# Three more places for weight blocks, and the first and last blocks of stages in two passes of six or seven

## The reference

```
x = x + 0.5*rms(swiglu(rms(x), w_gu, w_down))            # ffn1, hidden 2816
h = rms(x) @ w_in                                        # 14 columns of 128: xl 4, g 4, q 4, k 1, v 1
y = [rg_lru(conv(xl)) * gelu(g), window_attention(q, k, v)]   # each rms-normed
x = x + rms(y @ w_o)
x = x + 0.5*rms(swiglu(rms(x), ...))                     # ffn2
# block 2: layer_norm after each part, modulated by ada = silu(c) @ ada_w
x, ctx = retention over ctx + x (4 heads), then swiglu ffn3 on both
# block 3: only the latent
x = neighbourhood attention (16 heads, keys from x and ctx), then swiglu ffn4
```

## Time and profile before

| | |
|---|---|
| median of 3 runs | 3118.19 us (3117.08 to 3118.38) |
| the profiled execution, its own time | 3121.12 us |
| its span, first to last instruction | 3119.3 us |
| PE busy | 2943.9 us (94%) |
| DVE, ACT, POOL busy | 1505.9, 1048.2, 619.3 us |
| mean granted clock of PE | 0.97 |
| read from HBM | 262.54 MB |

### The profile page before, as it was taken

How to read it: one execution, slowest core, us unless ns; L and a number is a source line. 1 busy time by engine, 2 the same in 40 slices (tenths; PEclk the granted TensorE clock), 3 DMA queues, 4 the chain that set the end, 5 groups by cost and what they waited for, 6 DMA issues and landing times.

```text
span 3119.3 us, 39774 instructions
## 1 busy us (share of the span) xinstructions
PE 2943.9 (94%) x15968; PEld 2482.4 (80%) x15968; DVE 1505.9 (48%) x2524; ACT 1048.2 (34%) x1814; POOL 619.3 (20%) x330
## 2 busy tenths in 40 slices
PE   7999977889999999999999899999998999899997
PEld 6888965678878887868686788888896777878887
DVE  4667575555766424233232835445555535632224
ACT  4322235543232522122222541122236535442222
POOL 2333212113323110101011011111102212112221
PEclk9999998889999999999999899999998999999999
DMA  3444321014444210102011023223312111122221
GB/s 140 166 146 168 115 76 48 28 56 168 144 160 135 85 65 34 65 15 77 27 68 41 28 67 124 87 82 122 115 55 85 64 57 51 55 74 103 96 100 55
DMA packets 84697, 268.80 MB, mean 86 GB/s; under 512 B 8993, under 2 KB 16545, under 8 KB 84129
## 3 DMA queue, kind: packets, MB, share of 16 engines
q1 hardware_dynamic: 84512, 266.25, 25.0%
HBM read 262.54 MB, written 2.10 MB: 85 GB/s over the span
## 4 chain that ended last, share of the span: by engine, by line
PE 81%; DVE 10%; ACT 4%; issue 3%; POOL 1%; DMA 1%; SPq 0%; DVEq 0%; ACTq 0%; POOLq 0%
PE ps L1175 24%; PE ps L1176 24%; PE ps L1177 24%; PE ps L1362 3%; DVE t_misc L1827 2%; ACT t_whi L1444 1%; PE ps L1353 1%; DVE t_wlo L1737 1%; PE ps L1385 1%; PE ps L1412 1%; DVE t_misc L1757 1%; PE ps L1396 1%; POOL t_wlo L2166 1%; DMA t_x<-in_ctx 1%; PE ps L1265 1%
## 5 line engine op out<-in xcount | busy, mean ns | idle before, releaser
L1175 PE MATMUL ps<-t_h,t_whi 128*128 128x512 f32 (+1 forms) x2736 | 977.9, 357 | 56.2 <-DVE t_wlo L1737 29.1
L1176 PE MATMUL ps<-t_h,t_wlo 128*128 128x512 f32 (+1 forms) x2736 | 969.8, 354 | 0.0
L1177 PE MATMUL ps<-t_h,t_whi 128*128 128x512 f32 (+1 forms) x2736 | 968.7, 354 | 0.0
L2166 POOL TENSOR_TENSOR t_wlo<-t_raw,t_whi 128x1024 fp32r<-128x1024 f32 (+3 forms) x201 | 486.0, 2418 | 2083.4 <-ACT t_whi L1444 2083.4
L1175 PEld LDWEIGHTS ps<-t_h,t_whi 128*128 128x128 f32 x2736 | 527.2, 193 | 132.4 <-issue 23.0
L1737 DVE TENSOR_TENSOR t_wlo<-t_raw,t_whi 128x1024 fp32r<-128x1024 f32 (+3 forms) x201 | 253.1, 1259 | 687.3 <-ACT t_whi L1444 687.1
L1176 PEld LDWEIGHTS ps<-t_h,t_wlo 128*128 128x128 f32 x2736 | 527.2, 193 | 69.2 <-issue 1.0
L1177 PEld LDWEIGHTS ps<-t_h,t_whi 128*128 128x128 f32 x2736 | 526.6, 192 | 69.8
L1175 PE MATMUL ps<-t_hid,t_whi 128*128 128x256 f32 (+1 forms) x1648 | 536.4, 325 | 14.1 <-DVE t_hid L1869 8.5
L1444 ACT CAST t_whi<-t_raw 128x1024 fp32r<-128x1024 f32 (+3 forms) x402 | 402.1, 1002 | 402.6 <-PE ps L1177 379.0
L1176 PE MATMUL ps<-t_hid,t_wlo 128*128 128x256 f32 (+1 forms) x1648 | 531.7, 323 | 0.0
(11 more groups left out here) (225 smaller groups left out, 2473.6 us busy)
## 6 DMA issues: line engine op xcount, KB each, us to landing
t_raw<-in_gu SPq DMA_DIRECT2D x176, 512.0 KB, 3.2
t_raw<-in_ada SPq DMA_DIRECT2D x96, 512.0 KB, 3.3
t_raw<-in_dn SPq DMA_DIRECT2D x48, 448.0 KB, 3.2
t_raw<-in_dn SPq DMA_DIRECT2D x28, 512.0 KB, 3.5
t_raw<-in_ret_v SPq DMA_DIRECT2D x16, 512.0 KB, 3.2
t_raw<-in_ret_qk SPq DMA_DIRECT2D x16, 512.0 KB, 3.2
t_raw<-in_ret_g SPq DMA_DIRECT2D x16, 512.0 KB, 3.1
t_raw<-in_ret_o SPq DMA_DIRECT2D x16, 512.0 KB, 3.6
```

What stands on the lines that cost most here:

```text
L1175: e.matmul(out, whi, xlo, start=first, stop=False, skip_group_check=shared)
L1176: e.matmul(out, wlo, xhi, start=False, stop=False, skip_group_check=shared)
L1177: return e.matmul(out, whi, xhi, start=False, stop=last, skip_group_check=shared)
L2166: e.tensor_tensor(m.WLO[:, j % NH, 0:n], m.RAW[:, it.raw % NR, 0:n], m.WHI[:, j % NH, 0:n], ALU.subtract).then_inc(*S["lo_pool"].of(j))
```

## The change

Three more places for weight blocks: 4 and 5 in the context's columns of H (four pieces of 256 columns each, high halves in H's high part and low halves in its low part), and 6 in those of X, which gets a second name with the rounded type, `XW`. They are in use from the start to the start of ffn2 and from the end of the neighbourhood attention's keys to the end. `give` puts a preparation into the list with its place and the event that frees it; `over` frees a place and gives it on, or closes it, if it is one of the three and the context is about to come (`closing`).

With them: the first pass of ffn1, ffn2 and ffn4 takes six blocks instead of four (four side by side, then two one after the other), over each half, and that of the mixer seven, the four xl columns and three queries. At the end of ffn1, of ffn4 and in w_o the first of the eight last blocks is taken over all 512 tokens, and the seven others over the first half and then over the second. Ffn2's and ffn3's ends, ffn3's start and the neighbourhood attention's output columns keep batches of four. PARTS1 becomes 6, 8, 8. In the mixer the last query, the key's and the value's columns stand between the convolutions. In the neighbourhood attention the second keys come one unit earlier, and the value rows for the second half of the heads use banks 0, 1, 6, 7, 0, 1.

```diff
-PARTS1 = (7, 7, 8)
+PARTS1 = (6, 8, 8)
...
+    def give(slot, after):
+        j = next(coming)
+        where[j] = slot
+        put("prep", j=j, slot=slot, after=after)
+
     def over(j, signal, key):
-        release[j] = (signal, key)
-        put("prep", j=j + NH)
+        slot = where[j]
+        if slot in closing:
+            closing.remove(slot)
+            closed[slot] = [(signal, key)]
+        else:
+            give(slot, [(signal, key)])
...
# by_steps: blocks past the fourth, one after the other
+            for (_, _, nk, src, outs), j in zip(specs[4:], held[4:]):
+                (_, emptier, post), = outs
+                b = bank()
+                g = put("mm", w=j, slot=where[j], base=0, nk=nk, src=src, t0=t0, n=n, bank=b, po=0, before=seat(b, emptier, len(items)))
+                tick(nk * (n + 32) / 800)
+                if si == len(segs) - 1:
+                    over(j, "ps", g.id)
+                post(g)
...
# ffn(..., first=6, whole=1, begun=None)
-                together(specs[:4], subs)
-                specs = specs[4:]
+                together(specs[:first], subs)
+                specs = specs[first:]
+                if begun:
+                    begun()
...
-                last = columns(specs, ends, batch=4)
+                if whole:
+                    columns(specs[:whole], segs)
+                last = columns(specs[whole:], ends, batch=len(specs) - whole if whole else 4)
...
# the mixer
-        together([spec(c, scaled(("xl", c), MX + c * 515 + 3)) for c in range(4)], SUB1)
+        def query(c):
+            return spec(8 + c, scaled(("q", c), MQ + c * 512, 0.125))
+
+        together([spec(c, scaled(("xl", c), MX + c * 515 + 3)) for c in range(4)] + [query(c) for c in range(3)], SUB1)
         lru = recurrences()
+        others = (query(3), spec(12, scaled(("k",), MK)), spec(13, scaled(("v",), MGA + 1536)))
         for c in range(4):
             if c == 0:
                 put("conv", c=0)
             if c < 3:
                 put("conv", c=c + 1)
-            columns([spec(8 + c, scaled(("q", c), MQ + c * 512, 0.125))], SEG1)
+                columns([others[c]], SEG1)
             lru_gates(c)
         next(lru)
-        columns([spec(12, scaled(("k",), MK))], SEG1)
         next(lru)
-        columns([spec(13, scaled(("v",), MGA + 1536))], SEG1)
...
-        last = columns([(("w_o", j), (SLOT,), DC, ("y",), [(0, "drain_act", o_post(j))]) for j in range(DC)], SUB1, batch=4)
+        specs = [(("w_o", j), (SLOT,), DC, ("y",), [(0, "drain_act", o_post(j))]) for j in range(DC)]
+        columns(specs[:1], SEG1)
+        last = columns(specs[1:], SUB1, batch=7)
...
# the neighbourhood attention
-                                           lambda tt: NVV + vslot(tt) * 512, (0, 1, 2, 3, 4, 5), banks=(0, 1))
+                                           lambda tt: NVV + vslot(tt) * 512, (0, 1, 2, 3, 4, 5), banks=(0, 1, 6, 7, 0, 1), early=2)
...
-                    if b == 2:
+                    if b == (2 if c else 1):
                         keys(half * 4 + c + 1)
+                        if (half, c) == (1, 2):
+                            for slot in (4, 5):
+                                give(slot, state["h_free"])
...
+        give(6, [("na_ps", ("o", 1, 15))])
...
# the main program, before ffn1
+    for slot in (4, 5, 6):
+        give(slot, [])
...
+              whole=0, begun=lambda: closing.update((4, 5, 6)))      # ffn2
...
+    def weight(self, part, slot, o, n):
+        if slot < NH:
+            return (self.WHI, self.WLO)[part][:, slot, o:o + n]
+        if slot < 6:
+            at = part * 6144 + ((slot - 4) * 4 + o // 256) * 768 + 512 + o % 256
+            return self.H[:, at:at + n]
+        at = (part * 4 + o // 256) * 768 + 512 + o % 256
+        return self.XW[:, at:at + n]
```

112 lines of the change are left out of this document (62 added, 50 removed).

## The result

The changed kernel takes **3106.95 us** (median of 6 runs, 3104.72 to 3112.54), the kernel before 3117.64 in the same comparison: a ratio of 0.9968, 95% interval 0.9955 to 0.9980. The gain is 10.7 us where 54 were forecast. It was the fastest of its six executions (3104.72 us), and the profiled one of before took 3121.12, above all of its six: 5.7 of the 16.4 us lie between executions, not between kernels.

A forecast was written before the change was run, and what follows sets the result against it. PE is busy 2943.9 of 3119.3 us; all loss lies at stage borders, as idle PE and lower clock. Terms -2.0 + 18.1 + 13.3 + 13.5 + 8.4 + 2.7 = 54.0 give 3064 us; own range 3050 to 3078, for all 3047 to 3090.

The forecast's parts named there:

- ffn1 to mixer: Border of ffn1 and mixer: seven groups of cover and earlier weight blocks remove most idle PE and lower-clock loss, +18.1 us.
- The other half of the same term (+6.4): Mixer, 437 to 512: the 2.16 us weight wait and the gate matmuls' 3.12 us wait for the convolution go, +6.4 us.
- the prediction's rival of the raw buffers: Rival, chance 0.03: the raw-block ring keeps three buffers, blocks come no faster, the waits only move; 3118 us.
- Start (-2.0): Start of ffn1: 3.8 us of loss goes, but three copies delay the squares, PE's sum at about 31.6; -2.0 us.
- a rival for seven ends: Rival, chance 0.05: GpSimd makes both low half and gate product, giving new waits at seven part ends, 45 us; 3109 us.
- Moved queries (3 of 0 to 10.8): Mixer: query columns moved ahead no longer let key and value columns cover the recurrences' chain; 3 us idle charged, 0 to 10.8.
- Mixer to ffn2: Border of mixer and ffn2: +18.6 us of waits go, less 5 for the attention's uncovered tail and 0.3 for two passes; +13.3.
- Attention over the grid: Waits of the third scores, second-half rows and fifth output block go, less 1 us for three preparations in a row; +13.5 us.
- Ffn4's start and the end (+8.4 and +2.7): Ffn4's start: idle and lower-clock loss gone, +8.4 us; end: last mean and its subtraction come earlier, one block whole, +2.7.
- The one of the mixer's chains (0.15): Rival, chance 0.15: recurrences give back all 10.8 us as idle and the attention's tail stands open with 12; 3079 us.
- GpSimd's hold on VectorE (0.10): Rival, chance 0.10: GpSimd subtractions at ffn1's and mixer's ends stall VectorE in the first half's chain, 11 us less; 3075 us.
- the rival on ffn2's two waits: Rival, chance 0.07: both GpSimd jam waits at ffn2's part ends vanish, 12.9 us more gain; 3051 us.

The follow-up runs named there:

- e4: Only the change's part from the attention over the grid on; ffn1, mixer and ffn2 as before, except parts of 6, 8 and 8: 3100.07 us, 0.9937.
- e13: Changed kernel, with ffn1 ending in three whole blocks and a row of five instead of seven: 3103.7 us, 0.9956.
- e9: e7, with ffn1 ending in three whole blocks and a row of five instead of seven: 3099.63 us, 0.9937.
- e6: Changed kernel, with the low half of every weight block made on VectorE, none on GpSimd: 3096.69 us, 0.9927.
- e3: Changed kernel, with the start's three weight copies put behind the fifth k step of ffn1, behind the first squares: 3105.38 us, 0.9954.
- e5: Changed kernel, with the second half's norm sum and the first half's own next norm sum put later in PE's queue: 3096.95 us, 0.9927.
- e7: e2, with w_o again in two batches of four, interlaced with the attention's last units, no block taken whole: 3105.85 us, 0.9958.
- e2: Changed kernel, with the mixer's columns (queries, key, value) back in the order of before: 3113.0 us, 0.9980.
- e10: e4, with the three further places also given in the middle of w_o, for ffn2; w_o in two batches of four: 3093.08 us, 0.9921.
- e8: e4, with row group copies ahead of the weight preparations (reaching the retention too) and one place given one block of heads later: 3117.23 us, 0.9993.
- e11: e4, with the copy put ahead of the four preparations only at the last row group between the halves of the heads: 3096.85 us, 0.9928.
- e14: Kernel before, with low halves on VectorE outside retention and attention over the grid, and the second half's norm sum at ffn2's end later: 3092.93 us, 0.9921.
- e12: e10, with low halves on VectorE outside retention and attention over the grid, and the second half's norm sum at ffn2's end later: 3068.84 us, 0.9840.

## Why the prediction was wrong

**The step that failed** is in the term for ffn1 to mixer (+18.1, measured 6.6 us the other way): "the second half's chain gets seven groups of cover. All but 1.5 goes: +15.3". The groups over the second half are the last work of ffn1; what they can cover is the first half's norm. The second half's norm starts behind the last of them, and its sum stands two k steps into the mixer, where it stood before. I counted what PE would have to do and not what VectorE had to do in the same time. VectorE's timeline of the changed kernel; L1935 takes a group's result out of PSUM:

```profile
377.58 0.42 DVE L1935 TENSOR_TENSOR t_misc<-t_misc,ps 128x256 f32<-128x256 f32 x1 [1.48 <-PE ps L1237]
379.98 1.23 DVE L1793 TENSOR_TENSOR t_h<-t_raw,t_h 128x1024 fp32r<-128x1024 f32 x1 [1.98 <-ACT t_h L1500]
...
383.87 0.41 DVE L1935 TENSOR_TENSOR t_misc<-t_misc,ps 128x256 f32<-128x256 f32 x1
...
386.24 2.27 DVE L1860 TENSOR_TENSOR t_x<-t_x,t_misc 128x256 f32<-128x256 f32 x1
...
395.24 0.42 DVE L1935 TENSOR_TENSOR t_misc<-t_misc,ps 128x256 f32<-128x256 f32 x1
...
397.49 2.38 DVE L1840 SCALAR_TENSOR_TENSOR t_h<-t_x,t_par,t_h 128x256 fp32r<-128x256 f32 x1
...
407.18 2.40 DVE L1813 TENSOR_TENSOR t_misc<-t_misc,t_tmp 128x256 f32<-128x256 f32 x3 [1.44 <-ACT t_tmp L1512]
409.51 0.41 DVE L1935 TENSOR_TENSOR t_misc<-t_misc,ps 128x256 f32<-128x256 f32 x1
410.40 0.42 DVE L1813 TENSOR_TENSOR t_misc<-t_misc,t_tmp 128x256 f32<-128x256 f32 x1 [0.48 <-ACT t_tmp L1512]
```

PE hands over a result every 2.9 us (24 matmuls of 0.12 us), but from 377.58 on VectorE takes one every 5.3 us ((409.51 - 377.58) / 6). Between two of them stand steps of the first half's norm, a preparation, and with every second one a stall beside GpSimd (2.27 and 2.38 us for 0.42 and 0.48). VectorE is busy for 23.7 of these 31.9 us; for most of the rest it waits for ScalarE's copies and squares, 0.5 to 2.0 us at a time. The backlog grows with each group of the row. Before, only three results were in it:

```profile
389.38 0.41 DVE L1879 TENSOR_TENSOR t_misc<-t_misc,ps 128x256 f32<-128x256 f32 x1
...
395.45 0.41 DVE L1879 TENSOR_TENSOR t_misc<-t_misc,ps 128x256 f32<-128x256 f32 x1
...
400.73 0.41 DVE L1879 TENSOR_TENSOR t_misc<-t_misc,ps 128x256 f32<-128x256 f32 x1
```

The last result was taken 6.3 us behind the mixer's first matmul; changed it is 12.7. Before, PE came to the second half's sum only behind its two waits for low halves, 13.8 us behind the mixer's first matmul, and found it ready. Changed, these waits are gone but for 1.53 us, and PE stands at the sum until 14.0, because the results come so late: the sum is where it was. Behind it the changed kernel loses more. The three fences show PE changed, VectorE changed and VectorE before:

```profile
413.73 1.87 PE L1323 MATMUL ps<-t_con,t_misc 128*128 128x1 f32 x8 [0.98 <-DVE t_misc L1813]
...
418.17 1.05 PE L1331 MATMUL ps<-t_tmp,t_con 128*128 128x128 f32 x4
```

```profile
413.79 0.48 DVE L1822 TENSOR_SCALAR t_tmp<-t_con,t_st 128x128 f32<-128x128 f32 x2
419.26 0.48 DVE L1853 SCALAR_TENSOR_TENSOR t_misc<-t_misc,t_par,ps 128x256 f32<-128x256 f32 x1 [4.99 <-PE ps L1331]
```

```profile
411.16 0.48 DVE L1766 TENSOR_SCALAR t_tmp<-t_con,t_st 128x128 f32<-128x128 f32 x2
412.45 0.48 DVE L1797 SCALAR_TENSOR_TENSOR t_misc<-t_misc,t_par,ps 128x256 f32<-128x256 f32 x1 [0.81 <-PE ps L1273]
```

VectorE has the second half's factor ready and waits 4.99 us, before 0.81, until PE spreads it over the partitions (L1331, before L1273). In PE's queue that matmul now stands behind the first half's own next sum and 12 product matmuls, at the lower clock level that followed the wait of 9.18. This spreading is a better landmark than the last result, since the chain goes through it. All times are from the mixer's first matmul, in us:

| kernel | last result taken | factor spread | fourth gate column | from the one to the other |
|---|---|---|---|---|
| before | 6.3 | 17.2 | 116.0 | 98.8 |
| e4, four places | 6.3 | 18.3 | 117.5 | 99.1 |
| e13, row of five | 9.8 | 15.7 | 118.9 | 103.2 |
| e9, row of five, old order | 9.8 | 15.7 | 118.5 | 102.8 |
| e6, no GpSimd | 11.1 | 19.8 | 118.1 | 98.3 |
| changed, row of seven | 12.7 | 21.3 | 122.6 | 101.3 |
| e3, row of seven | 12.7 | 21.3 | 124.2 | 102.9 |
| e5, sums later | 12.7 | 21.4 | 120.6 | 99.2 |
| e7, row of seven, old order | 12.7 | 21.3 | 123.9 | 102.6 |
| e2, row of seven, old order | 12.7 | 21.3 | 126.1 | 104.8 |

Taking most of PE's wait at the sums away (e5) does not bring the spreading forward and shortens the stretch by 2 us at most. A shorter row brings it 5.6 us forward and the column 3.7 (e13 against changed) and 5.4 (e9 against e7). So the stretch is bound by the chain of the second half's norm and what follows it, over VectorE, ScalarE and PE's own queue. That this chain binds and not PE's waits is shown; the part of it that runs through PE's queue is read from the traces. PE's losses of 16.8 us before were waits beside this chain, and taking their cause away left the chain as it was. Of the 6.6 us lost, 4.1 stand before the spreading. What follows it took 98.3 to 104.8 us, in most kernels with seven places more than in those with four, and why is not settled. The order of the columns is not it: old and new order lie as far apart as two profiles of one code (e9 and e13; e7 and e2 against changed and e3).

The other half of the same term (+6.4) failed as well. The 2.16 us went, but the 3.12 before the gates' matmuls became 5.00. ScalarE (first) and VectorE (second) of the changed kernel ahead of that wait, L1996 taking results and L2003 beginning the convolution:

```profile
455.03 1.05 ACT L1500 CAST t_whi<-t_raw 128x1024 fp32r<-128x1024 f32 x1 [3.95 <-DMA t_raw<-in_w_in]
457.29 1.05 ACT L1500 CAST t_whi<-t_raw 128x1024 fp32r<-128x1024 f32 x1 [1.21 <-DMA t_raw<-in_w_in]
459.49 1.05 ACT L1500 CAST t_whi<-t_raw 128x1024 fp32r<-128x1024 f32 x1 [1.15 <-DMA t_raw<-in_w_in]
```

```profile
460.64 1.32 DVE L1793 TENSOR_TENSOR t_wlo<-t_raw,t_whi 128x1024 fp32r<-128x1024 f32 x1 [2.56 <-ACT t_whi L1500]
461.88 0.74 DVE L1996 SCALAR_TENSOR_TENSOR t_misc<-ps,t_tmp 128x256 f32<-128x256 f32 x2
462.55 0.53 DVE L2003 TENSOR_SCALAR t_misc<-t_misc,t_par 128x512 f32<-128x512 f32 x1
```

When the pass over seven blocks has freed its places, only three raw buffers stand filled. Between 451 and 465 ScalarE waits five times for a block's load, 8.9 us in all (before once, 2.86 us, at 440.56), and VectorE's results and the convolution stand behind a subtraction that waits for such a copy. This is the prediction's rival of the raw buffers, at this one place. It fits the longer stretch behind the spreading, but no run had a fourth raw buffer, so that is not shown.

**Start (-2.0):** right in mechanism, e3 shows it. The sum came at 30.51 with 2.28 us idle, forecast 31.6 and 4.1; in its place ffn1 has a wait of 2.01 us at the end of its first part (101.93), which I had as a rival for seven ends. It came at one in ffn1. That ffn1 as a whole came out at +2.4 for +2.0 is in part luck: the mixer's first matmul lies 3.7 us apart in profiles of kernels with four places here (392.65 to 396.34).

**Moved queries (3 of 0 to 10.8):** the wait before the fourth gate column did grow (13.27, forecast 8 to 10), but e2 gives no gain for undoing it, and with a row of five both orders take the same (118.9 and 118.5).

**Mixer to ffn2 (+13.3, measured 4.4):** the tail of the attention was forecast at 5 and measured at 8 (e7 against e2 and the changed kernel). ffn2's start was forecast at 18.6, the largest single number of the sum, and it too was far too high. All of ffn2 gained 12.1, and about half of it comes from parts of 6, 8 and 8, which were put at nothing (e4, with these parts and four places, has 407.8 us for 413.6). The places and the two passes over six blocks bring 5.6 (402.2 in e10 for 407.8 in e4). The sums' waits of 3.74 and 2.47 us that are left have the form of the mixer's; that they have the same cause was not tried.

**Attention over the grid (+13.5, measured 6.1):** the third scores' wait went (0.47 and 0.51 us left of 3.20). The allowance of 1 us for "three preparations in a row" was the mis-sized one: it is 6.6 us of idle PE. ScalarE and VectorE of the changed kernel:

```profile
2552.93 1.05 ACT L1500 CAST t_whi<-t_raw 128x1024 fp32r<-128x1024 f32 x1 [0.31 <-PE ps L1237]
2555.83 1.04 ACT L1500 CAST t_whi<-t_raw 128x1024 fp32r<-128x1024 f32 x1 [1.85 <-DMA t_raw<-in_na_qk]
2556.79 0.58 ACT L1587 COPY t_misc<-ps 128x512 f32<-128x512 f32 x1
```

```profile
2633.95 2.54 DVE L1793 TENSOR_TENSOR t_h<-t_raw,t_h 128x1024 fp32r<-128x1024 f32 x1 [6.13 <-ACT t_h L1500]
2636.51 0.69 DVE L2163 CUSTOM_DVE_ANT_1 t_tmp<-ps,t_misc 128x512 f32<-128x512 f32 x1
```

The row copy that frees the bank for the scores stands behind a preparation that waits for its load: the 2.37 us before the rows moved to 3.31 behind them (e8 and e11, with the copy first, have 0.77 and about 1.05 there). The scores of 2637.97 stand behind a subtraction that takes 2.54 us beside GpSimd's, for 1.23 alone; this reading rests on the trace.

**Ffn4's start and the end (+8.4 and +2.7):** right, 8.8 and 2.4 measured. **Nothing** for the retention and ffn3: 3.8 us less, which is no more than executions differ by. The same stages took 1281.8 us in the changed kernel, 1284.5 in e4 and 1285.8 in e3 (the retention alone 653.3, 656.5 and 654.9).

**The rivals.** The one of the mixer's chains (0.15) named the right engine, for the recurrences and not for the norm, and stopped at 3079. GpSimd's hold on VectorE (0.10) was priced at 11 us; e6 gave 10, but mainly in ffn2, so that the figure is right by luck. In the changed kernel a VectorE instruction of 0.42 us took 2.27 beside GpSimd's subtraction (386.24), so a low half on GpSimd costs VectorE 1.9 us where making it itself costs 1.23. The Trainium skill (SBUF — State Buffer, "Who interferes with whom") has the two engines share a pair of ports that one of them locks for a whole instruction; the trace agrees. The windows of 700 to 1000, inside ffn2, in before and in e14:

```profile
700.00:1000.00 300.00, 291.20 (x1280) 240.92 (x1279) 192.37 (x242) 93.21 (x128) 102.15 (x47) 0.98 0.46 156
```

```profile
700.00:1000.00 300.00, 300.00 (x1404) 251.86 (x1403) 193.76 (x277) 96.26 (x134) 24.62 (x19) 1.00 0.47 159
```

With four places, and in this stretch everything else as before, GpSimd's 102 us of work become 25, VectorE's share hardly changes (192.4 and 193.8), and PE waits no more. The 3051 of the rival on ffn2's two waits is not reached either: of 4.17 and 4.36 us, 1.50 and 5.64 are left in the changed kernel; only with the low halves on VectorE both go (e6, e12, e14). What the rivals lacked is one that says: the chain behind the wait is the bound, and the wait only moves.

## What to carry to other kernels

A wait of the main engine at a border is worth its length only if nothing else is late by as much: before counting it as won, add up what each of the other queues has to do between the same two points, in order. More buffers let preparations run ahead, but in an in-order queue they stand before the results of the running stage: keep the rows short where a norm or an eviction is on the same engine (here a row of five or four, with the places filled earlier), and take the first blocks of the next stage in passes over each half, which was the part that paid (5.6 us in ffn2, 8.8 at ffn4's start). An engine beside which the critical one stalls is not free help. The low halves all on VectorE brought as much as the whole change (e6, 10 us). With one sum placed later, and GpSimd kept for the stages that got longer in e6, it was 26 us on the kernel before (e14).

## What was not expected of the hardware

The same kind of wait was followed by very different stretches at the lower clock level, in profiles of kernels that are alike up to there. PE idles 2.3 to 3.4 us at 30 in the kernels with the three copies at the start. Behind it stand 3.4 us at the lower level in the changed kernel, 6.8 in e7 and 10.2 in e5, and these do not go by the length of the wait (2.28, 3.35 and 2.56 us). The kernels without these copies idle 2.6 us at 50 instead: 3.4 us at the lower level followed in before, 6.8 in e4, and none at all in e8, e10 and e11. In e3, which has neither wait, 3.4 us followed the wait of 2.01 us at the end of ffn1's first part. The mixer's first matmul lies as much as 4.8 us apart (396.86, 398.97 and 401.62 in changed, e7 and e5). A wait's price in one profile is thus uncertain by several us, and stages are better compared from landmark to landmark than by the end.
